# A mixture-of-experts step on one Trainium2 core: seven experts' weights on chip, and expert rows added to the residual rows in memory

## What is computed

```python
x = x + g1 * mix
hn = rmsnorm(x, norm2_w) * (1 + sc2) + sh2
# router: top-1 group of 4, then top-2 of its 8 experts; w = group weight * softmax of the two
y = zeros
for e in range(32):                       # D_EXPERT = 256
    hdn = silu(hn @ expert_w_gate[e]) * (hn @ expert_w_up[e])
    y = y + combine[:, e:e+1] * (hdn @ expert_w_down[e])
x = x + g2 * y                            # g2 differs for latent and context tokens
y_out = rmsnorm(x, final_norm_w)
```

## Time and profile before

| what | value |
|---|---|
| median of 3 runs | 871.64 us (869.63 to 873.62) |
| the profiled execution, its own time | 873.66 us |
| its span, first to last instruction | 871.8 us |
| TensorE busy | 740.1 us (85%) |
| VectorE, ScalarE, GpSimd busy | 372.9, 166.7, 195.6 us |
| DMA | 181.12 MB, mean 208 GB/s |
| chain that ended last | TensorE 54%, DMA 24% |

### The profile page before, as it was taken

The page is one execution under the profiler, slowest core; times in us unless marked ns, Lnnn a source line. Parts: engine busy times, 40 slices in busy tenths (PEclk is TensorE's granted clock), DMA queues, the critical chain, the costliest instruction groups (busy, mean ns, idle before and its releaser), DMA issues.

```text
span 871.8 us, 11055 instructions
## 1 busy us (share of the span) xinstructions
PE 740.1 (85%) x4208; PEld 474.3 (54%) x4208; DVE 372.9 (43%) x738; ACT 166.7 (19%) x258; POOL 195.6 (22%) x238
## 2 busy tenths in 40 slices
PE   5989996999999999999699999898777776887800
PEld 0255453558888556677588874554444443544400
DVE  0080489677666767457523346321111111111147
ACT  2621322011332125113001110111001001010132
POOL 4010044132334003013200011233222222222213
PEclk9999898899999999999889999999989999988965
DMA  8943403323133535323471028399999999999363
GB/s 304 372 149 103 145 0 109 133 88 105 51 108 115 164 123 157 110 56 85 170 288 49 25 88 322 137 342 366 389 392 386 399 395 384 398 385 388 154 254 121
DMA packets 73654, 181.12 MB, mean 208 GB/s; under 512 B 10036, under 2 KB 47044, under 8 KB 65296
## 3 DMA queue, kind: packets, MB, share of 16 engines
q1 hardware_dynamic: 62656, 157.84, 49.2%
q0 software_dynamic: 6256, 12.83, 4.6%
q10 hardware_dynamic: 4704, 9.93, 3.1%
HBM read 172.64 MB, written 14.48 MB: 215 GB/s over the span
## 4 chain that ended last, share of the span: by engine, by line
PE 54%; DMA 24%; DVE 11%; issue 4%; ACT 2%; POOL 2%; SPq 2%; ACTq 1%; DVEq 0%; POOLq 0%
DMA weights<-in_expert_w_up 21%; PE bank L1550 17%; PE bank L1692 8%; PE bank L1739 5%; PE bank L1542 4%; DVE weights L1056 2%; PE bank L1755 2%; PE bank L1474 2%; PE bank L1578 2%; DMA weights<-in_w_ada 2%; PE bank L1663 2%; PE bank L1654 2%; SPq L488 1%; PE bank L1681 1%; DVE attention L1082 1%
## 5 line engine op out<-in xcount | busy, mean ns | idle before, releaser
L1550 PE MATMUL bank<-h_cols,weights 128*128 128x128 f32 (+3 forms) x672 | 189.7, 443 | 2.5 <-DVE small L1023 2.5
L1550 PEld LDWEIGHTS bank<-h_cols,weights 128*128 128x128 f32 (+1 forms) x672 | 103.1, 190 | 90.3 <-issue 87.2
L1739 PE MATMUL bank<-weights,h_cols 128*64 128x256 f32 x512 | 65.9, 415 | 27.5 <-DMA weights<-in_expert_w_up 27.5
L1739 PE MATMUL bank<-qkv_gates,h_cols 128*64 128x256 f32 x512 | 67.7, 423 | 25.1 <-DMA qkv_gates<-in_expert_w_up 23.9
L1380 DVE TENSOR_TENSOR attention<-attention,bank 128x128 f32<-128x128 f32 x32 | 9.2, 288 | 177.1 <-ACT attention L942 177.1
L1692 PE MATMUL bank<-weights,h_cols 128*128 128x256 f32 x320 | 72.8, 390 | 0.8 <-DVE h_cols L1186 0.8
L1542 PE MATMUL bank<-weights,h_cols 128*128 128x256 f32 x320 | 70.3, 380 | 0.0
L1739 PEld LDWEIGHTS bank<-qkv_gates,h_cols 128*64 128x64 f32 x512 | 45.1, 153 | 43.3 <-issue 32.6
L1739 PEld LDWEIGHTS bank<-weights,h_cols 128*64 128x64 f32 x512 | 43.7, 150 | 45.3 <-issue 28.9
L1692 PEld LDWEIGHTS bank<-weights,h_cols 128*128 128x128 f32 x320 | 62.5, 196 | 10.1 <-DVE h_cols L1186 1.2
L1542 PEld LDWEIGHTS bank<-weights,h_cols 128*128 128x128 f32 x320 | 60.4, 190 | 9.3 <-DVE attention L1040 0.8
(11 more groups left out here) (268 smaller groups left out, 917.2 us busy)
## 6 DMA issues: line engine op xcount, KB each, us to landing
weights<-in_w_ada SPq DMA_DIRECT2D x24, 1024.0 KB, 7.1
qkv_gates<-in_expert_w_gate SPq DMA_DIRECT2D x16, 1024.0 KB, 18.7
qkv_gates<-in_expert_w_up SPq DMA_DIRECT2D x16, 1024.0 KB, 26.5
qkv_gates<-in_expert_w_down SPq DMA_DIRECT2D x16, 1024.0 KB, 22.6
weights<-in_expert_w_gate SPq DMA_DIRECT2D x16, 1024.0 KB, 17.6
weights<-in_expert_w_up SPq DMA_DIRECT2D x16, 1024.0 KB, 27.5
weights<-in_expert_w_down SPq DMA_DIRECT2D x16, 1024.0 KB, 22.8
weights<-in_w_in SPq DMA_DIRECT2D x14, 1024.0 KB, 6.7
```

The source lines that it names most:

```text
L1550: ins = mm(ps[0:m, 0:hi - lo], wt[:, k, c * m:(c + 1) * m], hT[:, k, lo:hi], start=(k == 0), stop=(k == KC - 1))
L1739: ins = mm(bank[2 + n][j * SLOTS:(j + 1) * SLOTS, 0:2 * P], xte[n][:, k, :], exgu[b][:, :, k, j * P:(j + 1) * P], start=(k == 0), stop=(k ...
```

## The change

- **Seven places for weights** (`WEIGHTS = 7`) instead of four. The SBUF tiles are laid out anew: `qkv_gates_tables` (A) holds three, `weights_x_h` (B) three, and the attention tile G one, in which the routing has its scratch. SP loads experts 0 to 2 when the attention is through, 3 after the last product of the projection, 4 and 5 when X of the latent and of the context tiles is stored, 6 behind "dest" and the new job. The expert stage is written out without loops; the token buffers are three (`TOKS`) instead of four.
- **Residual rows in memory.** X doesn't stay on chip: ScalarE stores each tile behind its squares to `x3_dram`.
- **Weighting at the drain.** A third routing product (job `wslot`) gives each slot its routing weight; `ctxslot` says whether the slot holds a context token. Per expert, VectorE forms the row of g2 that belongs to each slot (`row_factors`), and `expert_rows` multiplies the PSUM rows by weight and g2 as it copies them.
- **Adding DMA.** `add_rows` issues an indirect DMA that adds the 128 half rows to `x3_dram` (`compute_op=ALU.add`). Before each add GpSimd waits for the add before it; the drain of expert e waits for add e-2.
- **Tail.** Five loads from `x3_dram`, squares, root, final scaling, store.

```diff
+WEIGHTS = 7
+TOKS = 3
+END_SLOT, OVER_SLOT, JUNK_SLOT = (NE - 7) % WEIGHTS, (NE - 6) % WEIGHTS, (NE - 5) % WEIGHTS
...
-            for b in range(2):
-                load_gate_up(b, b, gu_landed[b])
-                load_down(b, b, dn_landed[b])
+            sp.wait_ge(s_out, 16 * 2)
+            for e in range(3):
+                load_gate_up(e, e, gu_landed[e])
+                load_down(e, e, dn_landed[e])
...
             load_used(sp, len(LOADS) - 1)
-            sp.wait_ge(s_out, 16 * 2)
-            for b in range(2, 4):
-                load_gate_up(b, b, gu_landed[b])
-                load_down(b, b, dn_landed[b])
+            load_gate_up(3, 3, gu_landed[3])
+            load_down(3, 3, dn_landed[3])
+            dve.wait(sp, ("hn", LT - 1))
+            sp.wait_ge(x2_written, 16 * LT)
+            load_gate_up(4, 4, gu_landed[4])
+            load_down(4, 4, dn_landed[4])
+            dve.wait(sp, ("hn", CTX))
+            sp.wait_ge(x2_written_ctx, 16)
+            load_gate_up(5, 5, gu_landed[5])
+            load_down(5, 5, dn_landed[5])
+            dve.wait(sp, "dest")
+            is_filled(sp, ("wslot",))
+            load_gate_up(6, 6, gu_landed[6])
+            load_down(6, 6, dn_landed[6])
+            for e in range(WEIGHTS, NE):
+                b = e % WEIGHTS
+                sp.wait_ge(gu_filled, e - WEIGHTS + 1)
+                load_gate_up(e, b, gu_landed[b])
+                sp.wait_ge(y_filled, e - WEIGHTS + 1)
+                load_down(e, b, dn_landed[b])
...
-            sp.wait_ge(ys_written[0], n_over * 16 + 16 * (NE // 2))
-            sp.wait_ge(ys_written[1], 16 * (NE // 2))
-            picks = ys_dram.rearrange("(r h) n -> r (h n)", h=2)
+            sp.wait_ge(ys_added, n_over * 16 + 16 * NE)
             for t in range(TILES):
-                for k in range(2):
-                    sp.dma_start(yp[t][k], picks[k * T + t * P:k * T + (t + 1) * P, :]).then_inc(yp_landed[t][k], 16)
+                sp.dma_start(yo[t], x3_dram[t * P:(t + 1) * P, :]).then_inc(x3_landed[t], 16)
...
-            def scatter_rows(e, n, col):
+            def add_rows(e, n, col, added):
                 pool.wait_ge(y_ready, e + 1)
                 pool.sem_inc(scatters_begun, 1)
                 nc.gpsimd.tensor_copy(sidxc[n][:, :], sidx[:, col]).then_inc(sidxc_set, 1)
                 pool.wait_ge(sidxc_set, e + 1)
+                if added is not None:
+                    pool.wait_ge(ys_added, added)
                 pool.sem_inc(scatters_begun, 1)
-                pool.indirect_dma_start(ys_dram[:, :], bass.IndirectOffsetOnAxis(ap=sidxc[n][:, :].bitcast(U32), axis=0), yb[n], None,
-                                        bounds_check=2 * T * 2 - 1, oob_is_err=False).then_inc(ys_written[n], 16)
+                pool.indirect_dma_start(x3_dram.rearrange("t (h n) -> (t h) n", h=2),
+                                        bass.IndirectOffsetOnAxis(ap=sidxc[n][:, :].bitcast(U32), axis=0), yb[n], None,
+                                        bounds_check=2 * T - 1, oob_is_err=False, compute_op=ALU.add).then_inc(ys_added, 16)
...
+            for e in range(NE):
+                g = e + TOKS + 2
+                if g < NE:
+                    pool.wait_ge(xg_turned, g - TOKS + 1)
+                    gather_block(slice(g, g + 1), g % TOKS)
+                    gather_rows(g % TOKS, g + 1)
+                add_rows(e, e % 2, slice(e, e + 1), 16 * e if e else None)
...
                 act.done(f(mt[t % 2], X[:, t, :], ACT.Square, accum_out=ss[:, t:t + 1]), ("ss2", t))
+                sc.dma_start(x3_dram[t * P:(t + 1) * P, :], X[:, t, :]).then_inc(x2_written if t < LT else x2_written_ctx, 16)
...
+            def row_factors(e, n, is_ctx):
+                v.scalar_tensor_tensor(g2s[n], g2d, is_ctx, g2l, ALU.mult, ALU.add).then_inc(factors_ready, 1)
+
+            def expert_rows(e, n, added, weight):
+                dv.wait_ge(factors_ready, e + 1)
                 dv.wait_ge(y_filled, e + 1)
-                if written is not None:
-                    dv.wait_ge(ys_written[n], written)
-                v.tensor_copy(yb[n], bank[4 + n][:, :]).then_inc(y_ready, 1)
+                if added is not None:
+                    dv.wait_ge(ys_added, added)
+                v.scalar_tensor_tensor(yb[n], bank[4 + n][:, :], weight, g2s[n], ALU.mult, ALU.mult).then_inc(y_ready, 1)
...
             for t in range(TILES):
-                y1, y2 = yp[t]
-                dv.wait_ge(yp_landed[t][1], 16)
-                dv.wait_ge(y1_scaled, t + 1)
-                link(v.scalar_tensor_tensor(y2, y2, pickw[:, 1, t:t + 1], y1, ALU.mult, ALU.add))
-                link(v.tensor_tensor(y2, y2, g2b[int(t == CTX)], ALU.mult))
-                v.tensor_tensor(X[:, t, :], X[:, t, :], y2, ALU.add).then_inc(x3_ready, 1)
+                mean_squares(t)
                 if t >= 1:
-                    mean_squares(t - 1)
-            mean_squares(CTX)
-            for t in range(POOL_TILES, TILES):
-                final_rows(t)
+                    final_rows(t - 1)
+            final_rows(CTX)
```

More of the change, by code:

```diff
@@ L535, in _ @@
-            sp.dma_start(fnb, final_w.rearrange("(a n) -> a n", a=1).partition_broadcast(P)).then_inc(s_fin, 16)
-            with sp.Fori(1, NE // 4) as it:
-                for b in range(4):
-                    sp.wait_ge(gu_filled, 4 * it + b - 3)
-                    load_gate_up(4 * it + b, b, gu_landed[b])
-                    sp.wait_ge(y_filled, 4 * it + b - 3)
-                    load_down(4 * it + b, b, dn_landed[b])
-            dve.wait(sp, "dest")
+            sp.wait_ge(s_out, 16 * 2)
@@ L942, in silu @@
                 f(sil[n], bank[2 + n][:, 0:P], ACT.Silu).then_inc(sil_ready, 1)
-            def experts(it, first=False, last=False):
-                for b in range(4):
-                    e = 4 * it + b
-                    if not (last and b == 3):
-                        silu(e + 1, (b + 1) % 2, None if first and b == 0 else e)
-                        turned_tokens(e + 2, b % 2, e + 1)
             for h in range(2):
@@ L953, in _ @@
             turned_tokens(0, 0, None)
+            dve.wait(sc, "dest")
             silu(0, 0, None)
             turned_tokens(1, 1, None)
-            experts(0, first=True)
-            with sc.Fori(1, NE // 4 - 1) as it:
-                experts(it)
-            experts(NE // 4 - 1, last=True)
-            dve.wait(sc, "dest")
+            for e in range(NE - 1):
+                silu(e + 1, (e + 1) % 2, e if e else None)
+                if e + 2 < NE:
+                    turned_tokens(e + 2, e % 2, e + 1)
             n_over = sc.value_load(over[0:1, 0:1], min_val=0, max_val=MAX_OVER)
@@ L1406, in _ @@
             hidden_columns(0, 0, None)
-            experts(0, first=True)
-            with dv.Fori(1, NE // 4 - 1) as it:
-                experts(it)
-            experts(NE // 4 - 1, last=True)
+            row_factors(0, 0, ctxslot[:, 0:1])
+            for e in range(NE):
+                if e + 1 < NE:
+                    hidden(e + 1, (e + 1) % 2, e if e else None)
+                expert_rows(e, e % 2, 16 * (e - 1) if e >= 2 else None, wslot[:, e:e + 1])
+                if e + 1 < NE:
+                    hidden_columns(e + 1, (e + 1) % 2, e if e else None)
+                    row_factors(e + 1, (e + 1) % 2, ctxslot[:, e + 1:e + 2])
             n_over = dv.value_load(over[0:1, 0:1], min_val=0, max_val=MAX_OVER)
```

227 lines of the change are left out of this document (112 added, 115 removed).

## The result

| | before | after |
|---|---|---|
| median, range | 873.28 us (869.61 to 874.89, 7 runs) | 880.63 us (878.1 to 883.26, 7 runs) |
| ratio after to before | | 1.0091, 95% interval 1.0069 to 1.0114 |
| span of the profiled execution | 871.8 us | 881.4 us (its time: 883.26) |

The change makes the kernel about 0.9% slower, where 842.4 us had been forecast. The medians differ by 7.35 us, the two profiled spans by 9.6: the profiled execution of the kernel after is the slowest of its seven, 2.6 us over their median, so differences between single profiled executions are good to 2 or 3 us only.

A forecast was written before the change was run, and what follows sets the result against it. Reading 100 MB of expert weights bounds the kernel. First add at 574.0, 28.0 adds at 8.4 and 4.0 at 4.2 end at 825.8; plus 16.7 tail gives span 842.5, forecast 842.4 us, range 828 to 895.

The forecast's parts named there:

- the price of one link in the chain of adds: Expert stage, GpSimd: each add waits for the previous landing; 8.4 us per add under the weight stream, 4.2 idle.
- the routing gets longer: Routing before the expert stage: added products and drain delay the first turn of tokens to 559.1, costing 4.4 us.
- Loaded cycle: Expert stage while weights stream: add landing 8.3 us plus 0.1 hand-off, 8.4 us from add to add, 28.0 adds.
- the upper end of 14.1: Expert stage: dearest landing assumed for an add under load, a gather and then a scatter, 14.1 us.
- Idle cycle: Expert stage after the weight stream: 4.1 us landing plus 0.1 hand-off, 4.2 us per add, for 4.0 adds.
- Tail: From last add to end of span: five loads instead of ten and less work, 16.7 us instead of 36.3.
- Rival 2: Expert stage: the chain of adds becomes the bound and is slower than before, 881.8 us; chance 0.32.
- the point of 855: End of the expert stage: adds ending at 855 us or later make the kernel slower than before.
- two turns (12.5): Expert stage: an add's rows pass each engine in two portions, each waiting its turn, landing after 12.5 us.
- the tipping value of 11.1: Expert stage: loaded add landing of 11.1 us, with 4.2 idle, from which the kernel turns slower than before.
- Seven buffers: Expert weight loads: three more experts on chip early, so the saturated stretch is 27.7 us shorter.
- The add's traffic: DMA engines in the expert stage: one more read per add, 0.45 us per expert, 10.8 us over 24 experts.

The follow-up runs named there:

- groups apart: Kernel after with experts taken from four groups in turn, each add waiting for the add four before, not the one before: 859.7 us, ratio to before 0.9841.

## Why the prediction was wrong

**The step that failed is the price of one link in the chain of adds:** 8.4 us from add to add while the weights stream, where the trace has 10.0. The path was right: the forecast too had the adds end last, at 825.8 for 824.5. But the adds come to 862.6 by the dearer link, a later start and dearer links at the end.

The forecast sum was first add at 574.0, 28 loaded cycles of 8.4 and four idle ones of 4.2, tail 16.7, a span of 842.5. The profile has 581.15, then 24 cycles to 821.15 at 10.0, then 41.5 us for the last eight adds (5.2 each), tail 18.8: 881.4. The 38.9 us between them (38.2 between 842.4 and the median) are:

- **Start, +7.1 us.** The step "the routing gets longer" was right for what it costed (the warming matmuls do stand behind the drain on the path, and the order took 4.5 us), but it had 4.4 for 10.0 at the first turn. It left out the clearing of the buffers, an instruction on GpSimd that stood ahead of the routing before and stands beside it now, and that it should have costed against VectorE, took the warming at the price of a warm clock (3.67, found 6.25), and it dismissed ScalarE's wait for "dest" by looking at its end and not at the table load behind it. From first turn to first add come another 1.5: 16.5 us instead of 14.9.
- **Loaded cycle, +38.4.** 24 cycles at 10.0 instead of 8.4. The landing was 9.2 for 8.3, between the taken value and the upper end of 14.1; the hand-off from a landing to the next start was 0.86 for the assumed 0.1. The hand-off is the miss that could have been avoided: the earlier trace rows showed it, as the 0.91 and 0.88 us between a GpSimd copy and the scatter that waits for it.
- **Idle cycle, +7.9, and fewer adds under load, -16.8.** Eight adds of 5.2 instead of 4.2; but fewer adds fit under the stream, 24 for 28, though it ended at 820.6 for 809.2; so four more were at the idle pace, 4 x (8.4 - 4.2).
- **Tail, +2.1.** First tile usable 3.6 us after issue as forecast; the last scaling ends at 13.3 instead of 12.4 behind the last add, since GpSimd's root takes 1.5 us a tile and two of them stand in the chain, and the end behind it took 5.5 instead of 4.3.

7.1 + 38.4 + 7.9 - 16.8 + 2.1 = 38.7, the rest is rounding.

**Rival 2 happened, by another way.** The chain of adds binds, and it is slower than before; the adds end at 862.6, above the point of 855 that was named. But the landing is not two turns (12.5); with 9.2 it stays below the tipping value of 11.1. That value had been worked out with the forecast's start, a hand-off of 0.1 and 4.2 idle. With the measured start of 581.15, 5.2 idle and the forecast's 809 for the stream, 8.8 adds may be left, 23.2 in 228 us, a cycle of 9.8 and a landing of 9.0: the kernel's 9.2 lies above it. So start, hand-off and idle cycle brought the tipping point down to the landing that came. The chances were given as if the landing alone decided: a landing of 7.5 to about 10 was to give 836 to 863 us, and 9.2 came with 880.6. In the forecast's own terms (an estimate) a landing of 9.2 gives 854, still well faster; with the hand-off of 0.86 in both cycles it is 868.5; start, idle landing and tail bring the rest.

**Seven buffers: right in kind.** 23.4 us where the weights bind, for 27.7. **The add's traffic: right in kind, too small.** 15.7 us for 10.8. With adds of groups apart the last weights land at 822.4 where the forecast had 809.2: 4.4 of it from the start (563.45 for 559.1), 4.9 from the adds' traffic, 4.3 from what the buffers bring less, 13.6 for a gap of 13.2. So even without the chain the forecast was 17 us low (859.7 for 842.4).

**The add's second read.** The earlier trace rows gave half of 0.9 us an expert for a read as large as the scatter's. The Trainium skill ("Collectives: The Full Stack", the section on the bandwidth ceiling) says that a reducing DMA emits two source reads per chunk. By the forecast's reading of that rule an add costs 0.45 us an expert more than a scatter; the runs have 0.65.

**The held step.** The clearing that held VectorE ended within 0.02 us of the step it held (532.90 and 532.92). The Trainium skill ("SBUF — State Buffer", the section "Who interferes with whom", on the port pair that VectorE and GpSimd share) says that the loser is blocked for the whole instruction of the other and doesn't share; the trace agrees, 1.63 us instead of 0.17.

**What stays open.** Why an add takes 2.3 to 2.7 us longer to land than a scatter under load (9.2 to 9.6 against 6.9) is not settled: no run changed its size. Nor is why an earlier start lengthens the cycle, nor what brings TensorE's clock down in the routing in some of the kernels.

## What to carry to other kernels

A chain of dependent DMAs has a pace of landing (counted from the issue) plus hand-off, and it must be multiplied by all its links from the first one on; compare that with what else bounds the stage, and look whether the data really demands the order (here only within a group of experts, 20.9 us). An adding DMA saves a pass at the end and pays for it on the busy engines: at 0.65 us an expert, 15.7 in all, it cost more than the 11 us that it saved in the tail. An earlier start of a stage that a full stream bounds is worth the DMA time that it fills, and not its length. And every instruction that a change adds ahead of a critical start, even a clearing on an idle engine, is to be laid beside what runs there on the other engines.

## What the runs showed of the hardware

- An adding indirect DMA of 128 half rows of 2 KB: its instruction on GpSimd takes 1.58 us (scatter 1.02); it lands after 8.4 to 10.0 us beside a full weight stream (groups apart; scatter 6.4 to 8.4) and after 3.8 to 4.8 with idle engines (scatter 2.6); it takes the full stream from 388 to 364 GB/s.
- 0.82 to 0.86 us pass on GpSimd from the landing of one indirect DMA to the start of the next that waits for it.
- A VectorE step of 128x5 took 1.63 us instead of 0.17 beside a GpSimd memset of 64x3072; four steps that had started beside the same memset before it took 0.17 or 0.18.
- Eight records of warming matmul took 6.25 us instead of 3.67 behind a stretch in which TensorE had been busy for 1.52 of 4 us, at its lower clock (granted 0.50).
